# Two decoder layers with 32 SwiGLU experts on one core: a unit of expert weights becomes one expert's whole matrix

## The chip, the cores and the metric

The kernel runs on one core of a Trainium2 chip, in float32. The metric is the device time of one execution in microseconds (us), the median of several runs. The tensor engine (PE) multiplies, the vector engine (DVE) and the scalar engine (ACT) do elementwise work and copies out of PSUM, GpSimd (POOL) does small reciprocal roots, and the sync engine (SP) issues the large loads. Expert weights come from HBM through the core's 16 DMA engines into SBUF.

## The reference, cut to what matters

256 tokens of width 1024 go through two layers. Each layer has a mixer (three kinds in parallel), a cross-attention, and then a mixture of 32 experts, in which a token goes to two:

```python
h = rmsnorm(x, norm3_g[l])
x = x + hierarchical_moe(h, router_wg[l], router_bg[l], router_we[l], router_be[l],
                         exp_w1[l], exp_w3[l], exp_w2[l])

def run(args):
    xb, e = args
    return (jax.nn.silu(xb @ w1[e]) * (xb @ w3[e])) @ w2[e]
```

w1 and w3 are 1024 x 512 per expert, w2 is 512 x 1024: each of the three matrices of an expert has 2 MiB. All 32 experts' weights are read in each layer, 201 MB.

## The kernel before, in words

All engines run one program over `DEPTH` = 2 layers. The dense part of a layer (projections, attentions, state-space mixer) uses weights that SP loads in 18 units (`DENSE`). The expert part goes over 8 quads of 4 experts. With 32 token places per expert (`CAP`), four experts fill the 128 columns of PE side by side: each matmul on expert weights has a 128 x 32 stationary operand (the gathered tokens `XG`, or the hidden values `HIDT`) and a 128 x 512 moving operand (weights), and writes 32 rows of a bank. In the trace each such float32 matmul shows as two records.

Weights of a quad arrive in `MOE_UNITS` = 12 units of 2 MiB, 16 KB in each of the 128 partitions: units 0 to 3 are w1, 4 to 7 are w3, 8 to 11 are w2. In the kernel before, unit i of a matrix holds, for all four experts of the quad, two of the eight 128-row pieces of w1 or w3 (a quarter of w2), so that 4 runs of 4 KB land in each partition. The units go through `ring`, six slots (`SLOTS`), in a loop over quads.

What sets the order:

- **SP** (lines 498 to 524) issues the units in order. Before it loads unit n into a slot, it waits until `units_used` shows that the unit six places earlier has been used by PE (line 522). In the first quad of a layer (`head`), four units go to buffers of the dense part that are free by then (`SPARE_UNITS` 2, 3, 4, 5 in `conv_mem`, `fox_ssd`, `keys_values`, `proj_ht`; line 511), in the order `HEAD_ORDER`; its last two units, 10 and 11, wait for slots 0 and 1 (line 519). The next layer's first dense loads wait for `units_used` too (line 482).
- **PE** (function `quad`, lines 1543 to 1606) waits for a unit in `landed_unit`, runs the 16 matmul records on it, and adds 1 to `units_used` (lines 1580 and 1600). The token gathers of a quad (`gather`, 8 records of 128 x 128 each) stand partly before the first unit and partly between units 0, 1 and 2. After unit 7 come four transposes of the hidden values (line 1590), after unit 11 the scatter (8 records of 128 x 512) that gives the experts' outputs back to the tokens. The helper `mm` is line 1264, so nearly all of PE's work has this line.
- **DVE and ACT** scale the gathered tokens (line 1228), make the SwiGLU product (lines 811, 1236, 1238), copy results (lines 813, 817) and add to the tokens `X` (line 1245). DVE also makes the next quad's selection (line 1147).

Of the kernel before, what the change touches and what calls it, by code (L numbers as in the profile page):

```python
# [24 lines left out]
P = 128  # L25
DEPTH, S, D = 2, 256, 1024
NT = S // P
KC = D // P
# [4 lines left out]
QUAD = 4  # L33
# [150 lines left out]
def trunk(nc, a, out):  # L184
    with ExitStack() as ctx:
# [15 lines left out]
        ring = sb("ring", [P, SLOTS, UNIT])  # L201
# [57 lines left out]
        spare = (conv_mem[:, 0:UNIT], fox_ssd[:, 0:UNIT], keys_values[:, :], proj_ht[:, PROJ_HT - UNIT:])  # L259
# [41 lines left out]
        XG = view(proj, 0, KC, P)  # L301
# [5 lines left out]
        HIDT = view(sq, 512, 4, P)  # L307
# [25 lines left out]
        bank = [ctx.enter_context(nc.psum_tensor(f"bank{b}", [P, 512], F32)) for b in range(NB)]  # L333
        B_GATH, B_SELT, B_UP, B_HIDT, B_DOWN, B_SCAT = (0, 1), 2, (3, 4), 5, (6, 7), (0, 1, 3, 4)
# [4 lines left out]
        landed = [sem(f"landed{s}") for s in range(SLOTS)]  # L339
        spare_in = [sem(f"spare_in{i}", 16) for i in range(SHIFT)]  # L340
# [43 lines left out]
        units_used = sem("units_used")  # L384
# [66 lines left out]
        def landed_by(n, slot, head, l, quads):  # L451

            a_layer = DENSE_TURNS - SHORT[slot]
            layers = l * a_layer + DENSE_TURNS if head else (l + 1) * a_layer
            return layers + quads * MOE_TURNS + sum(moe_slot(m, head) == slot for m in range(n + 1))
# [4 lines left out]
        @block.sync  # L460
        def _(sp):
            for t in range(NT):
                sp.dma_start(X[:, t, :], a["x"][0, t * P:(t + 1) * P, :]).then_inc(x_in[t], 16)
            sp.dma_start(con[:, :], a["const"]).then_inc(const_in, 16)

            def dense(kind, i, l):

                name = {"kv": "xa_wkv", "wq": "xa_wq", "w_out": "w_out", "wo": "xa_wo"}.get(kind, "w_in")
                c0, w, _ = IN_COLS.get(kind, (C_XBC if kind == "xbc" else 0, 512, 0))
                w = W_FV if kind == "fv" else w  # L470
                rows = "a (c p) n -> p (a c) n" if kind in ("w_out", "wo") else "a (p c) n -> p (a c) n"
                v = a[name][bass.ds(l, 1)].rearrange(rows, c=KC)
                return w, v[:, :, c0 + i * 512:c0 + i * 512 + w]

            with sp.Fori(0, DEPTH) as l:

                sp.wait_ge(passes_known, at(passes_known, l, 1))
                quads_before = sp.snap(load_passes(sp, l) * NQ)
                for n, (kind, i) in enumerate(DENSE):
                    if n < SLOTS:  # L480

                        sp.wait_ge(units_used, quads_before * MOE_UNITS + LAST_IN_SLOT[n] + 1)
                        alone(sp)
                    else:

                        sp.wait_ge(*full(last_use(DENSE[n - SLOTS]), l))
                        alone(sp)
                    w, src = dense(kind, i, l)
                    if kind == "fv":
                        place = ring_view(n % SLOTS, IN_COLS["fv"][1])  # L490
                        dt = a["w_in"][bass.ds(l, 1)].rearrange("a (p c) n -> p (a c) n", c=KC)[:, :, C_DT:C_DT + SH]
                        sp.dma_start(place[:, :, w:], dt).then_inc(dt_in, 16)
                    else:
                        place = ring_view(n % SLOTS, w)
                    sp.dma_start(place[:, :, 0:w], src).then_inc(landed[n % SLOTS], 16)

                def quad(q, quads, head=False):
                    for n in HEAD_ORDER if head else range(MOE_UNITS):
                        name, i = ("exp_w1", "exp_w3", "exp_w2")[n // 4], n % 4
                        w = a[name][bass.ds(l, 1)].rearrange("a e k n -> (a e) k n")[bass.ds(q * QUAD, QUAD)]  # L500
                        if name == "exp_w2":
                            src = w.rearrange("e (p c) n -> p e c n", c=4)[:, :, i, :]
                        else:
                            src = w.rearrange("e (p c) n -> p e (c n)", c=KC)[:, :, i * 1024:(i + 1) * 1024]
                        slot = moe_slot(n, head)
                        if slot is None:
                            i = SPARE_UNITS.index(n)

                            sp.wait_ge(*full((("kv", 3, 1), ("ysT", NT - 1), ("xo", 1, XH - 1), ("router",))[i], l))
                            alone(sp)  # L510
                            sp.dma_start(spare[i].rearrange("p (e n) -> p e n", e=QUAD), src).then_inc(spare_in[i], 16)
                            continue
                        if head and n < SLOTS + SHIFT:

                            sp.wait_ge(*full(last_use(DENSE[len(DENSE) - SLOTS + slot]), l))
                            alone(sp)
                        elif head:

                            sp.wait_ge(units_used, quads * MOE_UNITS + MOE_UNITS + slot + 1)
                        else:  # L520

                            sp.wait_ge(units_used, quads * MOE_UNITS + SLOTS + n + 1)
                        sp.dma_start(ring[:, slot, :].rearrange("p (e n) -> p e n", e=QUAD), src  # L523
                                     ).then_inc(landed[slot], 16)
                moe_quads(sp, l, quad, head=lambda q, quads: quad(q, quads, head=True))
            tiles_added = sp.snap(load_passes(sp, DEPTH) * (NQ * NT))
            for t in range(NT):

                sp.wait_ge(x_added, tiles_added + t + 3 - NT)
                alone(sp)  # L530
                sp.dma_start(out[0, t * P:(t + 1) * P, :], X[:, t, :]).then_inc(x_out, 16)
            sp.wait_ge(x_out, 16 * NT)
# [729 lines left out]
        def _(pe):  # L1262
            def mm(dst, lhsT, rhs, start=True, stop=True):
                return nc.tensor.matmul(dst, lhsT, rhs, start=start, stop=stop)  # L1264

            pe.wait_ge(const_in, 16)
            with pe.Fori(0, DEPTH) as l:
# [62 lines left out]
                for i in range(4):  # L1330
                    job = ("xbc", i)
                    w = arrived(("xbc", i // 2))
# [209 lines left out]
                def quad(q, quads, head=False):  # L1542


                    def landed_unit(n):
                        slot = moe_slot(n, head)
                        if slot is None:
                            i = SPARE_UNITS.index(n)
                            pe.wait_ge(spare_in[i], at(spare_in[i], l, 16))
                            return spare[i].rearrange("p (e c n) -> p e c n", e=QUAD, n=512)  # L1550
                        pe.wait_ge(landed[slot], landed_by(n, slot, head, l, quads) * 16)
                        return ring[:, slot, :].rearrange("p (e c n) -> p e c n", e=QUAD, n=512)

                    pe.wait_ge(sel_ready, quads + 1)
                    sel = SEL.rearrange("p t e s -> p t (e s)")
# [13 lines left out]
                    for n in range(8):  # L1569
                        if n < 4:  # L1570

                            pe.wait_ge(XG_ready, quads * 4 + n + 1)
                        u = landed_unit(n)
                        for c in range(2):
                            k = n % 4 * 2 + c
                            for e in range(QUAD):
                                r = slice(CAP * e, CAP * (e + 1))
                                last = mm(bank[B_UP[n // 4]][r, :], XG[:, k, r], u[:, e, c, :],
                                          start=k == 0, stop=k == KC - 1)
                        last.then_inc(units_used, 1)  # L1580
                        if n < 2:
                            gather(n + 2)
                        if n == 3:
                            pe.wait_ge(selg_ready, quads + 1)
                            for t in range(NT):
                                last = nc.tensor.transpose(bank[B_SELT][:, t * P:(t + 1) * P], selg[:, t, :], ident)  # L1586
                            last.then_inc(selt_full, 1)
# [3 lines left out]
                    last.then_inc(hidt_full, 1)  # L1591
                    pe.wait_ge(HIDT_ready, quads + 1)
                    for n in range(4):
                        u = landed_unit(8 + n)
                        for c in range(2):
                            for e in range(QUAD):
                                r = slice(CAP * e, CAP * (e + 1))
                                last = mm(bank[B_DOWN[c]][r, :], HIDT[:, n, r], u[:, e, c, :],
                                          start=n == 0, stop=n == 3)
                        last.then_inc(units_used, 1)  # L1600
                    pe.wait_ge(SELT_ready, quads + 1)
                    pe.wait_ge(YS_ready, quads + 1)
                    for i in range(4):
# [69 lines left out]
```

## Time and profile before

| | before |
|---|---|
| median of 3 runs | 1596.47 us (1595.89 to 1597.43) |
| span of the profiled execution | 1589.7 us |
| PE busy | 1185.8 us, 75% |
| DVE busy | 321.3 us, 20% |
| ACT busy | 221.5 us, 14% |
| moved by DMA | 476.65 MB |

The span runs from the first to the last instruction of the profiled execution. That execution's own device time is not given beside it; the median of the runs is 6.8 us above its span. The page shows the span in 40 slices, the chain of work that ended last, and groups of instructions with the idle time before them; the trace gives the same for any stretch.

### The profile page before, as it was taken

Reading aid. Unit: us, or ns where it says so; the run is one execution under the profiler, and the core shown is the slowest. Engines: PE = TensorE matmul, PEld = TensorE weight load, DVE = VectorE, ACT = ScalarE, POOL = GpSimd, SP = SyncE. Lnnn points to the kernel's source line nnn. Section 1 sums busy time; section 2 is a strip of 40 time slices with the busy share of each in tenths; the row PEclk is TensorE's granted clock in tenths of the full one; section 3 lists DMA queues with packets and bytes.
Section 4 is the critical chain, followed back from the end, with each engine's and each line's share of the span. In section 5 each row is a group of like instructions: output and inputs, shape, how many; then the busy total and the mean of one; then the engine's idle time right before and its main releaser. Section 6 shows DMA issues by size and latency. Waiting matters only on the chain.

```text
span 1589.7 us, 16075 instructions
## 1 busy us (share of the span) xinstructions
PE 1185.8 (75%) x6030; PEld 557.3 (35%) x6031; DVE 321.3 (20%) x835; ACT 221.5 (14%) x491; POOL 43.9 (3%) x81
## 2 busy tenths in 40 slices
PE   6999898977656656566579998988776566566565
PEld 4765544442212212112147645445322122122121
DVE  1125613131101101101021256131311011011010
ACT  4124312110000000000031243122000000000000
POOL 0110000000000000000001100000000000000000
PEclk9999999989989889889889999999798889789888
DMA  9563145379999999999974631453799999999997
GB/s 350 159 212 107 54 158 198 120 274 409 409 410 410 410 410 410 410 410 410 371 250 124 212 107 53 159 211 119 276 410 409 410 409 410 409 410 410 409 410 288
DMA packets 143333, 476.65 MB, mean 300 GB/s; under 512 B 6358, under 2 KB 14894, under 8 KB 143278
## 3 DMA queue, kind: packets, MB, share of 16 engines
q1 hardware_dynamic: 141616, 472.62, 77.0%
q10 hardware_dynamic: 1662, 3.32, 0.6%
q8 instruction: 32, 0.52, 0.1%
q14 instruction: 23, 0.19, 0.0%
HBM read 474.87 MB, written 1.05 MB: 299 GB/s over the span
## 4 chain that ended last, share of the span: by engine, by line
PE 45%; DMA 42%; DVE 5%; issue 3%; SPq 2%; ACT 2%; DVEq 0%; ACTq 0%
PE bank L1264 43%; DMA ring<-exp_w 42%; SPq L523 2%; PE bank L1280 2%; DMA ring<-w_in 1%; DVE X L1245 1%; ACT fox_ssd L817 0%; ACT Y L606 0%; DVE proj_ht L1147 0%; DVE fox_ssd L979 0%; ACT SCO L778 0%; DVE smax L1112 0%; ACT H L766 0%; DVE fox_ssd L1051 0%; DVE proj_ht L1029 0%
## 5 line engine op out<-in xcount | busy, mean ns | idle before, releaser
L1264 PE MATMUL bank<-ring,proj_ht 128*32 128x512 f32 (+3 forms) x2432 | 439.7, 650 | 151.9 <-DMA ring<-exp_w 149.7
L1264 PEld LDWEIGHTS bank<-ring,proj_ht 128*32 128x32 f32 (+1 forms) x2432 | 153.3, 133 | 384.1 <-issue 189.8
L1264 PE MATMUL bank<-ring,SCO 128*32 128x512 f32 x1024 | 165.7, 784 | 114.0 <-DMA ring<-exp_w 112.6
L1264 PEld LDWEIGHTS bank<-ring,SCO 128*32 128x32 f32 x1024 | 34.6, 129 | 234.4 <-DMA ring<-exp_w 148.1
L1264 PE MATMUL bank<-ring,conv_mem 128*128 128x512 f32 x256 | 114.6, 601 | 1.1 <-DVE Y L1061 1.1
L1264 PE MATMUL bank<-ring,H 128*128 128x512 f32 x256 | 112.3, 594 | 2.6 <-ACT H L606 1.5
L1245 DVE TENSOR_TENSOR X<-X,bank 128x512 f32<-128x512 f32 x64 | 44.0, 688 | 338.0 <-PE bank L1264 338.0
L1264 PE MATMUL bank<-proj_ht,H 128*128 128x128 f32 x512 | 73.4, 294 | 23.9 <-DVE proj_ht L1147 23.9
L1264 PEld LDWEIGHTS bank<-proj_ht,H 128*128 128x128 f32 x512 | 64.0, 200 | 62.6 <-DVE proj_ht L1147 35.8
L1264 PE MATMUL bank<-fox_ssd,proj_ht 128*128 128x512 f32 (+1 forms) x160 | 62.5, 600 | 20.6 <-ACT fox_ssd L817 20.6
L1264 PEld LDWEIGHTS bank<-ring,H 128*128 128x128 f32 x256 | 47.8, 190 | 59.5 <-issue 59.4
L1238 DVE SCALAR_TENSOR_TENSOR SCO<-Y,bank 128x512 f32<-128x512 f32 x16 | 16.9, 1054 | 254.7 <-PE bank L1264 254.7
L1264 PEld LDWEIGHTS bank<-ring,conv_mem 128*128 128x128 f32 x256 | 48.3, 192 | 56.8 <-issue 56.6
L1264 PE MATMUL bank<-proj_ht,ring 128*128 128x256 f32 x256 | 55.7, 380 | 0.0
L817 ACT COPY fox_ssd<-bank 128x512 f32<-128x512 f32 x32 | 17.2, 589 | 270.8 <-PE bank L1264 270.8
L1264 PEld LDWEIGHTS bank<-proj_ht,ring 128*128 128x128 f32 x256 | 48.5, 190 | 6.5
L813 ACT COPY SCO<-bank 128x512 f32<-128x512 f32 x16 | 9.4, 585 | 295.1 <-PE bank L1590 295.1
L1228 DVE TENSOR_TENSOR proj_ht<-bank,g 128x256 f32<-128x256 f32 x64 | 27.2, 425 | 111.8 <-PE bank L1264 111.8
L808 ACT COPY proj_ht<-bank 128x256 f32<-128x256 f32 x16 | 6.0, 372 | 313.5 <-PE bank L1586 295.2
L1264 PEld LDWEIGHTS bank<-fox_ssd,proj_ht 128*128 128x128 f32 (+1 forms) x160 | 24.0, 174 | 60.0 <-issue 60.0
L606 ACT COPY proj_ht<-bank 128x512 f32<-128x512 f32 (+2 forms) x32 | 15.4, 480 | 129.1 <-PE bank L1264 128.9
L1236 DVE SCALAR_TENSOR_TENSOR Y<-Y,bank 128x512 f32<-128x512 f32 x16 | 11.0, 688 | 97.8 <-ACT Y L811 97.8
(189 smaller groups left out, 812.1 us busy)
## 6 DMA issues: line engine op xcount, KB each, us to landing
ring<-exp_w SPq DMA_DIRECT2D x184, 2048.0 KB, 23.7
ring<-w_in SPq DMA_DIRECT2D x8, 2048.0 KB, 17.8
ring<-xa_wkv SPq DMA_DIRECT2D x8, 2048.0 KB, 11.9
ring<-w_out SPq DMA_DIRECT2D x4, 2048.0 KB, 9.8
ring<-xa_wq SPq DMA_DIRECT2D x4, 2048.0 KB, 9.2
ring<-xa_wo SPq DMA_DIRECT2D x4, 2048.0 KB, 7.7
ring<-w_in SPq DMA_DIRECT2D x6, 1024.0 KB, 12.3
conv_mem<-exp_w SPq DMA_DIRECT2D x2, 2048.0 KB, 12.7
```

The costliest lines, as they stand in the source:

```text
L523: sp.dma_start(ring[:, slot, :].rearrange("p (e n) -> p e n", e=QUAD), src).then_inc(landed[slot], 16)
L606: nc.scalar.copy(dst, src).then_inc(read(job), 1)
L808: nc.scalar.copy(SELT, bank[B_SELT][:, 0:S]).then_inc(SELT_ready, 1)
L813: nc.scalar.copy(HIDT, bank[B_HIDT][:, :].rearrange("p (c s) -> p c s", c=4)).then_inc(HIDT_ready, 1)
L817: last = nc.scalar.copy(YS[:, n * 512:(n + 1) * 512], bank[B_DOWN[n]][:, :])
L1228: v.tensor_tensor(XG[:, 2 * i:2 * i + 2, :], view(bank[B_GATH[i % 2]], i // 2 * 2 * P, 2, P), bc(my_gain[:, 2 * i:2 * i + 2], 2, P), ALU.m ...
L1236: step(v.scalar_tensor_tensor(SIGM, SIGM, 1.0, bank[B_UP[0]][:, :], ALU.add, ALU.mult))
L1238: v.scalar_tensor_tensor(HID, SIGM.rearrange("p (q c) -> p c q", c=4), 0.5, bank[B_UP[1]][:, :].rearrange("p (q c) -> p c q", c=4), ALU.mu ...
L1245: last = v.tensor_tensor(x, x, bank[B_SCAT[i]][:, :], ALU.add)
L1264: return nc.tensor.matmul(dst, lhsT, rhs, start=start, stop=stop)
L1280: last = nc.tensor.transpose(bk(job)[0:src.shape[1], i * P:i * P + src.shape[0]], src, ident[0:src.shape[0], 0:src.shape[0]])
```

## The change

A unit is now one expert's whole matrix, contiguous in HBM, and lands as one run of 16 KB in each partition. PE needs all four experts for a matmul step, so it waits for the four units of a matrix ahead of the first step, and gives the four slots back together after the last. The matmuls themselves, their number, shapes and order over k and the experts, stay as they were; so do the slots, the order in which units are loaded, and SP's wait conditions.

```diff
                 def quad(q, quads, head=False):
                     for n in HEAD_ORDER if head else range(MOE_UNITS):
-                        name, i = ("exp_w1", "exp_w3", "exp_w2")[n // 4], n % 4
-                        w = a[name][bass.ds(l, 1)].rearrange("a e k n -> (a e) k n")[bass.ds(q * QUAD, QUAD)]
-                        if name == "exp_w2":
-                            src = w.rearrange("e (p c) n -> p e c n", c=4)[:, :, i, :]
-                        else:
-                            src = w.rearrange("e (p c) n -> p e (c n)", c=KC)[:, :, i * 1024:(i + 1) * 1024]
+                        name = ("exp_w1", "exp_w3", "exp_w2")[n // QUAD]
+                        w = a[name][bass.ds(l, 1)].rearrange("a e k n -> (a e) k n")[bass.ds(q * QUAD + n % QUAD, 1)]
+                        src = w.rearrange("e (p c) n -> p (e c n)", p=P)
...
-                        sp.dma_start(ring[:, slot, :].rearrange("p (e n) -> p e n", e=QUAD), src
+                        sp.dma_start(ring[:, slot, :], src
                                      ).then_inc(landed[slot], 16)
...
+                    def landed_matrices(matrix, width):
+
+                        return [landed_unit(QUAD * matrix + e, width) for e in range(QUAD)]
...
-                        u = landed_unit(n)
+                        if n % 4 == 0:
+                            u = landed_matrices(n // 4, 512)
                         for c in range(2):
                             k = n % 4 * 2 + c
                             for e in range(QUAD):
                                 r = slice(CAP * e, CAP * (e + 1))
-                                last = mm(bank[B_UP[n // 4]][r, :], XG[:, k, r], u[:, e, c, :],
+                                last = mm(bank[B_UP[n // 4]][r, :], XG[:, k, r], u[e][:, k, :],
                                           start=k == 0, stop=k == KC - 1)
-                        last.then_inc(units_used, 1)
+                        if n % 4 == 3:
+                            last.then_inc(units_used, QUAD)
...
                     for n in range(4):
-                        u = landed_unit(8 + n)
+                        if n == 0:
+                            u = landed_matrices(2, 1024)
                         for c in range(2):
                             for e in range(QUAD):
                                 r = slice(CAP * e, CAP * (e + 1))
-                                last = mm(bank[B_DOWN[c]][r, :], HIDT[:, n, r], u[:, e, c, :],
-                                          start=n == 0, stop=n == 3)
-                        last.then_inc(units_used, 1)
+                                last = mm(bank[B_DOWN[c]][r, :], HIDT[:, n, r],
+                                          u[e][:, n, c * 512:(c + 1) * 512], start=n == 0, stop=n == 3)
+                        if n == 3:
+                            last.then_inc(units_used, QUAD)
```

SP, in the loop over quads, the last four units of a quad. Before (each row `L522` is the arithmetic of a wait, each DMA one unit of 4 runs of 1024 numbers per partition):

```order
L522 REGISTER_ALU
L523 DMA ring<-exp_w 128x4x1024
L522 REGISTER_ALU
L523 DMA ring<-exp_w 128x4x1024
L522 REGISTER_ALU
L523 DMA ring<-exp_w 128x4x1024
L522 REGISTER_ALU
L523 DMA ring<-exp_w 128x4x1024
```

And now:

```order
L519 REGISTER_ALU
L520 DMA ring<-exp_w 128x4096
L519 REGISTER_ALU
L520 DMA ring<-exp_w 128x4096
L519 REGISTER_ALU
L520 DMA ring<-exp_w 128x4096
L519 REGISTER_ALU
L520 DMA ring<-exp_w 128x4096
```

The loads stand in the same places with one long run each; 166 rows of SP before and after.

PE, the same loop, w3 and w2 of a quad (`SCO` holds the hidden values, `proj_ht` the gathered tokens; rows L1551 before and L1550 after are in `landed_unit`; here a float32 matmul counts once). Before:

```order
L1551 ISA
L1264 MATMUL bank<-ring,proj_ht 32x512 x16
L1551 ISA
L1264 MATMUL bank<-ring,proj_ht 32x512 x16
L1590 MATMUL bank<-con,SCO 128x128 x4
L1264 MATMUL bank<-ring,SCO 32x512 x16
L1551 ISA
L1264 MATMUL bank<-ring,SCO 32x512 x16
```

And now:

```order
L1550 ISA x2
L1261 MATMUL bank<-ring,proj_ht 32x512 x32
L1596 MATMUL bank<-con,SCO 128x128 x4
L1550 ISA
L1261 MATMUL bank<-ring,SCO 32x512 x32
```

The waits that stood among the matmuls of a matrix have moved ahead of all 32 of them.

## Rows read from the trace of the kernel before

**Rows 1.** The page: DMA share and GB/s in 40 slices of the span.
```profile
DMA  9563145379999999999974631453799999999997
GB/s 350 159 212 107 54 158 198 120 274 409 409 410 410 410 410 410 410 410 410 371 250 124 212 107 53 159 211 119 276 410 409 410 409 410 409 410 410 409 410 288
```

**Rows 2.** The page: the chain that ended last, by engine.
```profile
PE 45%; DMA 42%; DVE 5%; issue 3%; SPq 2%; ACT 2%; DVEq 0%; ACTq 0%
```

**Rows 3.** Timeline, PE in quad 1 of layer 1 (start us, us, engine, line, operation).
```profile
483.90 3.67 PE L1264 MATMUL bank<-fox_ssd,proj_ht 128*128 128x512 f32 x8 [1.29 <-ACT fox_ssd L817]
...
506.28 3.43 PE L1264 MATMUL bank<-ring,proj_ht 128*32 128x512 f32 x16 [2.73 <-DMA ring<-exp_w]
...
511.41 1.92 PE L1264 MATMUL bank<-ring,proj_ht 128*32 128x512 f32 x16 [1.70 <-DMA ring<-exp_w]
...
545.34 3.67 PE L1264 MATMUL bank<-fox_ssd,proj_ht 128*128 128x512 f32 x8 [1.29 <-ACT fox_ssd L817]
```

**Rows 4.** DMA packets from 28 to 36, 38 to 44 and 500 to 520 us.
```profile
DMA packets 1518, 3.09 MB, mean 386 GB/s; under 512 B 16, under 2 KB 16, under 8 KB 1517
...
DMA packets 2070, 2.09 MB, mean 348 GB/s; under 512 B 32, under 2 KB 2069, under 8 KB 2070
...
DMA packets 2062, 8.19 MB, mean 410 GB/s; under 512 B 62, under 2 KB 62, under 8 KB 2062
```

**Rows 5.** DMA from 5.5 to 6.5 us, SP's queue (packets, MB): it loads `con`.
```profile
q1 hardware_dynamic: 43, 0.22, 59.0%
```

**Rows 6.** A unit issued at 317.96 us; DMA just after (PEclk, DMA share, GB/s last).
```profile
317.96 0.37 SPq L523 DMA_DIRECT2D ring<-exp_w  x1
...
DMA to landing us min/median/max: 8.2/8.2/8.2
...
318.00:319.20 1.20, 1.20 (x13) 1.20 (x12) 0.53 (x1) 0.58 (x1) 0.00 (x0) 1.00 0.30 38
```

**Rows 7.** The load into `proj_ht` issued at 324.45 us: time to landing.
```profile
DMA to landing us min/median/max: 8.0/8.0/8.0
```

**Rows 8.** Timeline of quad 0 of layer 1, and unit 4 of quad 1.
```profile
335.69 1.99 PE L1264 MATMUL bank<-ring,proj_ht 128*32 128x512 f32 x16
...
337.75 103.36 SPq L523 DMA_DIRECT2D ring<-exp_w  x22
...
343.38 1.90 PE L1264 MATMUL bank<-fox_ssd,proj_ht 128*32 128x512 f32 x16
...
345.86 1.92 PE L1264 MATMUL bank<-keys_values,proj_ht 128*32 128x512 f32 x16
...
349.32 3.62 PE L1264 MATMUL bank<-ring,proj_ht 128*32 128x512 f32 x32
...
355.44 8.77 PE L1264 MATMUL bank<-ring,SCO 128*32 128x512 f32 x64 [0.67 <-ACT SCO L813]
...
372.72 1.92 PE L1264 MATMUL bank<-ring,proj_ht 128*32 128x512 f32 x16
...
383.41 1.93 PE L1264 MATMUL bank<-ring,proj_ht 128*32 128x512 f32 x16 [0.80 <-DMA ring<-exp_w]
```

**Rows 9.** Stretches: us, busy PE, PEld, DVE, ACT, POOL; PEclk, DMA share, GB/s.
```profile
356.50:359.70 3.20, 3.20 (x19) 0.64 (x13) 0.00 (x0) 0.00 (x0) 0.00 (x0) 0.50 1.03 415
359.90:364.20 4.30, 4.30 (x43) 1.04 (x32) 0.00 (x0) 0.00 (x0) 0.00 (x0) 1.00 1.02 412
...
506.60:509.90 3.30, 3.11 (x16) 0.44 (x8) 0.00 (x0) 0.00 (x0) 0.00 (x0) 0.50 1.02 408
```

**Rows 10.** Timeline at the end of layer 1 and the start of layer 2.
```profile
786.45 0.62 SPq L492 DMA_DIRECT2D ring<-w_in  x1
...
787.77 1.92 PE L1264 MATMUL bank<-ring,SCO 128*32 128x512 f32 x16 [1.59 <-DMA ring<-exp_w]
...
790.98 3.67 PE L1264 MATMUL bank<-fox_ssd,proj_ht 128*128 128x512 f32 x8 [1.29 <-ACT fox_ssd L817]
...
810.16 5.22 PE L1264 MATMUL bank<-ring,proj_ht 128*128 128x268 f32 x22
```

More of the change, by code:

```diff
@@ L510, in quad @@
                             alone(sp)
-                            sp.dma_start(spare[i].rearrange("p (e n) -> p e n", e=QUAD), src).then_inc(spare_in[i], 16)
+                            sp.dma_start(spare[i], src).then_inc(spare_in[i], 16)
                             continue
@@ L1542, in quad, with landed_unit @@
                 def quad(q, quads, head=False):
-                    def landed_unit(n):
+                    def landed_unit(n, width):
                         slot = moe_slot(n, head)
@@ L1549, in landed_unit @@
                             pe.wait_ge(spare_in[i], at(spare_in[i], l, 16))
-                            return spare[i].rearrange("p (e c n) -> p e c n", e=QUAD, n=512)
-                        pe.wait_ge(landed[slot], landed_by(n, slot, head, l, quads) * 16)
-                        return ring[:, slot, :].rearrange("p (e c n) -> p e c n", e=QUAD, n=512)
+                            u = spare[i]
+                        else:
+                            pe.wait_ge(landed[slot], landed_by(n, slot, head, l, quads) * 16)
+                            u = ring[:, slot, :]
+                        return u.rearrange("p (c n) -> p c n", n=width)
+                    def landed_matrices(matrix, width):
+                        return [landed_unit(QUAD * matrix + e, width) for e in range(QUAD)]
                     pe.wait_ge(sel_ready, quads + 1)
```

## The prediction

> **What bounds the kernel now.** I read the page's slices first. In the dense part of a layer the DMA engines are half idle; in the expert part, slices 10 to 19 and 30 to 39, they move 409 to 410 GB/s without a break [rows 1]. The chain of waits agrees: PE 45%, DMA 42% [rows 2], PE's share lying mostly in the dense part. The timeline of a quad shows it at close range: PE runs 16 records on a unit, then waits for the next, every 5.12 us (506.28 to 511.41) [rows 3]. A quad, from scatter to scatter, takes 545.34 - 483.90 = 61.44 us, which is 12 units of 5.12 us. So in the expert part only two things can change the time: how fast the DMA engines move bytes, and whether they ever run out of issued loads. They do not now, since each unit's slot is given back 2 to 3.5 us after it landed.
>
> **Term 1, the longer runs.** The mean packet was 3.09 MB / 1518 = 2 KB at 386 GB/s, 1 KB at 348, 4 KB at 410 [rows 4]. Over 16 engines that is 47.1 ns for 1 KB, 84.9 ns for 2 KB, 159.8 ns for 4 KB. Each doubling leaves a fixed part: 2 x 47.1 - 84.9 = 9.3 ns, 2 x 84.9 - 159.8 = 10.0 ns. I take 9.3. If a run of 16 KB is one packet, it takes 4 x 159.8 - 3 x 9.3 = 611 ns, so 429 GB/s, and a unit (2.097 MB) 4.90 us instead of 5.12. Does a long run stay whole? While SP loaded `con`, its queue moved 0.22 MB in 43 packets, 5.1 KB each [rows 5]: nothing cuts at 4 KB there. The bounds are 4.90 us and, if runs are cut, 5.12 us. Alone this term would give 12 x 0.22 = 2.6 us per quad, 42 us over 16 quads.
>
> The Trainium skill (DMA: Bandwidth & Descriptors, "Where 436 GB/s comes from") puts the ceiling of this path at 435 GB/s. By that a unit takes 4.82 us at best and the sum below would be some 7 us lower; the 429 is under it.
>
> **Term 2, slots given back by four.** The ring has six slots. When the last unit of a matrix has landed, four slots hold that matrix, and only two loads are issued beyond it. Nothing more can be issued until PE has finished all 64 records. Two units keep the DMA engines busy for 9.8 us (10.2 at the old rate). A load issued to idle engines landed 8.2 us and 8.0 us after its issue (38 GB/s were moving in the first 1.2 us) [rows 6, 7]. Against 5.12 us of pure transfer that is 2.9 us of start and finish; I add 0.1 us from PE's last record to SP's issue (335.69 + 1.99 = 337.68, issue at 337.75 [rows 8]). So, with T the time from a matrix's landing to its last matmul, the next matrix lands after the larger of T + 3.0 and two units, plus two units more.
>
> What is T? The nearest rows are in quad 0, where the units lay ready. For w1 the records ran from 335.69 to 343.38 + 1.90 = 345.28: 9.6 us, with two gathers and their copies in between. For w3: 345.86 to 349.32 + 3.62 = 352.94, 7.1 us. For w2: 8.77 us [rows 8], because the granted clock was 0.50 (1.2 GHz) in its first part and 1.00 (2.4 GHz) after [rows 9]. Sixteen records take 1.92 us at full clock and 3.43 us at half [rows 3]. After a wait of 2.73 us the clock fell to 0.50 within the burst at 506.28 [rows 3, 9]. In the changed kernel PE idles far longer ahead of w3 and w2, so I take 8.8 for both, and 9.6 for w1, since its gathers run shortly before. The bounds are 9.6, 7.1, 7.1 at full clock throughout, and 11.3, 10.5, 10.5 if half clock lasts twice as long in each as in the burst at 355.44.
>
> A quad then takes (9.6 + 3.0) + (8.8 + 3.0) + (8.8 + 3.0) = 36.2 us, plus six units of 4.90 = 29.4: 65.6 us against 61.4. At 5.12 us a unit: 66.9.
>
> **Term 3, the edges of a layer.** Quad 0's units 10 and 11 are issued when w1 is finished, 345.4 instead of 337.75, and land at 353.2 and 358.1. So w2 starts at 358.1 instead of 355.44 [rows 8] and ends at 366.9. The four loads that wait for it follow at 367.0, and quad 1's w1 is complete at 367.0 + 2.9 + 2 x 4.90 = 379.7. Before, it was one unit ahead of the wait that ended at 383.4 [rows 8], 378.3: +1.4. Six whole quads follow: 6 x 4.2 = +25.2. In the last quad w1 to w3 to w2 takes 12.6 + 11.8 + 4 x 4.90 = 44.0 instead of 8 x 5.12 = 41.0: +3.0. Then the last burst is 8.8 us, where one unit took 2.0 [rows 10]: +6.8, with nothing to hide it, as copies, scatter and the next layer's norms follow on it. Sum 36.4 us per layer, 73 us for both.
>
> **What costs nothing.** The next layer's first loads were issued at 786.45, 4.5 us ahead of the last scatter; now they come 1.2 us ahead of it, since the slots are given back at the burst's end. PE first uses them near 810 [rows 10], 19 us after the scatter; this slack covers 3.3 us, and if it were gone the price would be those 3.3 us once. SP's queue has the same loads in the same order, so nothing is moved past another load. Gathers, transposes and DVE's work are as before: after w2's burst, copies, scatter, selection and gather take 372.7 - 364.2 = 8.5 us [rows 8], and 8.8 + 8.5 is less than the 21.6 us until the next w1 is complete.
>
> **The sum.** The profiled span is 1589.7 us; with 73 it is 1663. The median of the runs stands 6.8 us above this span, so I forecast 1596.5 + 73 = **1669 us**.
>
> **Rivals.**
>
> - *Runs are cut or gain nothing* (20%). Rows 5 speak against it. A quad takes 66.9 us, the layer's edges +2.2, +3.9 and +6.8, so 2 x (6 x 5.5 + 12.9) = 92: 1688 us.
> - *The clock stays half for longer* (15%). In the bursts after 10 us of idling T may be 11.3, 10.5 and 10.5: a quad 14.3 + 13.5 + 13.5 + 29.4 = 70.7, +9.3. Layer: 6 x 9.3 + 3 + 6.4 + 8.5 = 74, so 1744 us in full; half of the effect gives 1706. For it: a wait of under 3 us is followed by half clock now [rows 3, 9]. Against it: full clock came back inside the burst at 355.44.
> - *The burst keeps full clock* (10%). T is 9.6, 7.1, 7.1. A quad takes 12.6 + 10.1 + 10.1 + 29.4 = 62.2, +0.8; the edges -0.3, +1.3 and +5.1. Sum 2 x 11 = 22: 1618 us. The Trainium skill (TensorE: Matmul & The Clock Gate, "HAM oscillation") advises to run all k-tiles before the next DMA wait so that PE stays warm, which would speak for this change; here the half-clock row ahead of it makes me give it little.
> - *Faster: the restart is hidden* (5%). The place is SP's wait at line 523. If part of the 2.9 us is hidden because four loads are issued at once, the DMA engines never starve; this decides when T + restart is under 9.8 us, so with a restart under 1.0 us at w3 and w2 and 0.2 us at w1. Then a quad takes 12 x 4.90 = 58.8, -2.6; last quad 39.2 instead of 41.0, -1.8; last burst +6.8. 2 x (-15.6 - 1.8 + 6.8) = -21: 1575 us. Against it stand 8.0 and 8.2 us from issue to landing.
> - *The longer runs are slower* (5%): at 380 GB/s a unit takes 5.5 us, a quad 36.2 + 33.0 = 69.2, the sum near 126: 1722 us.
>
> **How the numbers follow.** My forecast has 45%, with its own range 1650 to 1685. A measurement of this kernel can tell about 0.2% (3 us) from no change. Faster: 5% from the hidden restart and 1% for a full clock together with a better rate than 429. Within 0.2%: 2%, where a full clock meets a short restart. Slower: the rest, 92%. The range is 1618 to 1712: it holds the forecast, the cut runs, the full clock, and the smaller half of the clock rival; outside are the faster case, the slower runs and a clock at half for most of the bursts.
>
> **What would show each step.** DMA packets of 16 KB and about 429 GB/s in a stretch in which DMA is busy. The DMA share in the expert slices below 1.00, with gaps after each pair of units, three in a quad. Bursts of 64 records on PE near 8.8 us for w3 and w2, and waits of PE on `ring<-exp_w` of about 13 us. Scatter to scatter 65.6 us. SP waiting for PE at its line for the loads, with 8 us from issue to landing of the first of four. The forecast is wrong if the DMA share stays at 1.03 through a quad (no starving), if packets are still 4 KB, or if the 64 records take over 10 us.

## The result and the profile after

The changed kernel takes 1719.6 us (median of 4 runs, 1716.2 to 1721.6) against 1596.2 for the kernel before, measured beside it: 1.077 times the kernel before, 95% interval 1.075 to 1.0785. The sign and the mechanism came out as forecast, the size did not: 123 us slower where 73 were forecast, and 8 us beyond the upper end of the range.

The page of the changed kernel, the lines that answer to [rows 1] and [rows 2]:

```profile
span 1718.4 us, 16107 instructions
...
PE   6999898764655645546579999988745546455455
...
PEclk9999999887878868878789999998868778688787
DMA  9472133589898898988673621335988888999885
GB/s 350 121 241 103 50 134 160 196 345 375 352 376 368 373 390 353 376 366 351 261 251 115 228 99 49 147 147 196 371 350 352 365 363 355 384 375 379 367 349 215
...
PE 59%; DMA 32%; DVE 3%; issue 2%; SPq 1%; ACT 1%; DVEq 0%; ACTq 0%
```

In the expert slices the DMA engines moved an unbroken 410 GB/s before; now it is mostly 350 to 390, with busy digits of 8 and 9. The chain has moved from DMA (42% before) to PE (59%), although PE has the same work.

SP's own waits, from the same trace (who waited for whom: us in total, times, longest us):

```profile
SPq L520 <- PE bank L1261: 900.1, 46, 23.8
```

SP waits 46 times for PE at its line for the loads, close to once per matrix (48), up to 23.8 us each. PE waits for the landings in turn. The timeline of quad 2 of layer 1 with the start of the next (start us, us), which answers to [rows 3]. The quads of a layer are numbered 0 to 7 by the order of their scatters; [rows 3] lie in quad 3 by this count, not in quad 1:

```profile
442.44 3.67 PE L1261 MATMUL bank<-fox_ssd,proj_ht 128*128 128x512 f32 x8 [1.28 <-ACT fox_ssd L814]
447.79 2.05 PE L1261 MATMUL bank<-proj_ht,H 128*128 128x128 f32 x16 [1.68 <-DVE proj_ht L1144]
454.30 3.42 PE L1261 MATMUL bank<-ring,proj_ht 128*32 128x512 f32 x16 [4.46 <-DMA ring<-exp_w]
457.65 1.16 PE L1261 MATMUL bank<-proj_ht,H 128*128 128x128 f32 x8
458.74 1.92 PE L1261 MATMUL bank<-ring,proj_ht 128*32 128x512 f32 x16
460.59 1.16 PE L1261 MATMUL bank<-proj_ht,H 128*128 128x128 f32 x8
461.68 3.64 PE L1261 MATMUL bank<-ring,proj_ht 128*32 128x512 f32 x32
...
478.44 8.45 PE L1261 MATMUL bank<-ring,proj_ht 128*32 128x512 f32 x64 [12.76 <-DMA ring<-exp_w]
...
499.84 9.68 PE L1261 MATMUL bank<-ring,SCO 128*32 128x512 f32 x64 [11.13 <-DMA ring<-exp_w]
510.81 3.67 PE L1261 MATMUL bank<-fox_ssd,proj_ht 128*128 128x512 f32 x8 [1.28 <-ACT fox_ssd L814]
...
522.86 3.27 PE L1261 MATMUL bank<-ring,proj_ht 128*32 128x512 f32 x16 [4.68 <-DMA ring<-exp_w]
```

Scatter to scatter is 510.81 - 442.44 = 68.4 us (forecast 65.6, before 61.4). T, the time from a matrix's landing to its last matmul, is read here from its first record to its last: 461.68 + 3.64 - 454.30 = 11.0 us for w1, 8.45 for w3, 9.68 for w2. The waits on `ring<-exp_w` are 12.8 and 11.1 us.

Stretches of this kernel: the burst of w2 that began at 431.37, first and later part; then the gap in the loads after a w1 (busy times; PEclk, DMA share, GB/s last):

```profile
431.40:437.00 5.60, 5.60 (x28) 1.52 (x32) 0.00 (x0) 0.00 (x0) 0.00 (x0) 0.51 1.01 430
437.00:441.00 4.00, 4.00 (x40) 1.08 (x32) 0.00 (x0) 0.00 (x0) 0.00 (x0) 1.00 0.69 295
...
465.50:467.00 1.50, 0.19 (x2) 0.00 (x0) 0.37 (x1) 0.87 (x2) 0.00 (x0) 1.00 0.62 131
```

While loads are in flight they move at 430 GB/s; 429 was worked out from [rows 4]. Half clock holds for 5.6 us of the burst, and DMA runs dry before the burst has ended. SP's issues after the burst of w2 (it ended at 431.37 + 9.79 = 441.16), and the time from the first of them to its landing:

```profile
441.42 1.49 SPq L520 DMA_DIRECT2D ring<-exp_w  x3
...
DMA to landing us min/median/max: 7.8/7.8/7.8
```

So 0.26 us from PE to the issue, and 7.8 to the landing, of which 4.9 are transfer. After the burst of w3 before it (issue at 418.63) and the w1 after it (465.38) the first load landed 7.7 and 8.0 us after its issue, and SP issued it 0.06 us after PE's last record. From the end of w2 at 441.16 to the next w1 at 454.30 are 13.1 us: two units of 4.9 and 3.3 us of restart, not 3.0.

### The profile page after: what moved, and what is told of

Same layout as the page of the kernel before. It is cut to its first block, busy times and chain, and to the rows that moved or that the text cites. A ratio compares the mean times of both kernels' runs of the same rounds, so it can differ in the third digit from the quotient of the medians.

```text
span 1718.4 us, 16107 instructions
## 1 busy us (share of the span) xinstructions
PE 1172.9 (68%) x6030; PEld 581.4 (34%) x6031; DVE 321.3 (19%) x835; ACT 221.9 (13%) x491; POOL 43.5 (3%) x81
## 4 chain that ended last, share of the span: by engine, by line
PE 59%; DMA 32%; DVE 3%; issue 2%; SPq 1%; ACT 1%; DVEq 0%; ACTq 0%
PE bank L1261 57%; DMA ring<-exp_w 31%; PE bank L1277 2%; SPq L520 1%; DMA ring<-w_in 1%; ACT Y L603 0%; DVE fox_ssd L976 0%; ACT SCO L775 0%; ACT H L763 0%; DVE fox_ssd L1048 0%; DVE proj_ht L1026 0%; ACT proj_ht L697 0%; DVE smax L1109 0%; DVE fox_ssd L1050 0%; DVE proj_ht L934 0%
## 5 line engine op out<-in xcount | busy, mean ns | idle before, releaser
L1261 PE MATMUL bank<-ring,proj_ht 128*32 128x512 f32 (+3 forms) x2432 | 446.9, 652 | 243.5 <-DMA ring<-exp_w 241.1
L1261 PEld LDWEIGHTS bank<-ring,proj_ht 128*32 128x32 f32 (+1 forms) x2432 | 167.6, 138 | 452.7 <-issue 440.7
L1261 PE MATMUL bank<-ring,SCO 128*32 128x512 f32 x1024 | 154.2, 769 | 163.6 <-DMA ring<-exp_w 163.6
L1261 PEld LDWEIGHTS bank<-ring,SCO 128*32 128x32 f32 x1024 | 42.1, 137 | 265.0 <-issue 265.0
L1261 PE MATMUL bank<-fox_ssd,proj_ht 128*128 128x512 f32 (+1 forms) x160 | 73.8, 602 | 20.5 <-ACT fox_ssd L814 20.5
L1261 PEld LDWEIGHTS bank<-ring,H 128*128 128x128 f32 x256 | 47.8, 190 | 59.5 <-issue 59.4
L1225 DVE TENSOR_TENSOR proj_ht<-bank,g 128x256 f32<-128x256 f32 x64 | 27.2, 425 | 199.9 <-PE bank L1261 199.9
L1261 PE MATMUL bank<-keys_values,proj_ht 128*128 128x256 f32 (+1 forms) x96 | 33.7, 488 | 2.0 <-DVE proj_ht L853 2.0
## 6 DMA issues: line engine op xcount, KB each, us to landing
ring<-w_out SPq DMA_DIRECT2D x4, 2048.0 KB, 10.2
```

The lines of the kernel that those rows point to most:

```text
L1225: v.tensor_tensor(XG[:, 2 * i:2 * i + 2, :], view(bank[B_GATH[i % 2]], i // 2 * 2 * P, 2, P), bc(my_gain[:, 2 * i:2 * i + 2], 2, P), ALU.m ...
```

## The experiments

### Grouping alone, with 4 KB runs

The kernel before, with PE's waits and the return of slots in fours (`group4k`):

```diff
-                        u = landed_unit(n)
+                        if n % 4 == 0:
+                            four = [landed_unit(n + j) for j in range(4)]
+                        u = four[n % 4]
...
-                        last.then_inc(units_used, 1)
+                        if n % 4 == 3:
+                            last.then_inc(units_used, 4)
```

(and likewise for w2). Three dots mark lines left out.

> The kernel before with its 4 KB runs; PE alone is changed: it waits for the four units of a matrix and gives their slots back together. Theory A (starving by slots given back in fours): each matrix costs T + about 3.3 us + two units, with T 11.0, 8.5 and 9.7 us as in the changed kernel, so a quad takes 29.2 + 9.9 + 6 x 5.12 = 69.8 us and the whole some 20 us more than the changed kernel's 1719.6, about 1740. Theory B (what costs is the long run itself: a slower restart or uneven DMA engines): a quad stays near 61.4 us plus little, the whole below 1640.

It took 1747.9 us, 1.095 times the kernel before (1.093 to 1.096). From its scatters at 445.02 and 869.22 us the six quads between take 70.7 us each. Its timeline shows the same bursts behind the same waits:

```profile
483.07 8.94 PE L1264 MATMUL bank<-ring,proj_ht 128*32 128x512 f32 x64 [13.11 <-DMA ring<-exp_w]
...
505.36 9.74 PE L1264 MATMUL bank<-ring,SCO 128*32 128x512 f32 x64 [11.51 <-DMA ring<-exp_w]
```

The loss comes with PE's grouping alone, with not one long run in the kernel. The long runs help: the changed kernel is 28 us faster than this one. The forecast of 1740 us and 69.8 us per quad was 8 and 0.9 us low.

### Waiting for four, giving back one by one

The same kernel, but `units_used` rises after each unit's 16 records, as in the kernel before (`wait4k`; only the first half of the diff above).

> As the last, but each unit's slot is given back after its own 16 matmul records, as before. Theory A: the first slot comes back under 3.5 us after the matrix landed, with 10.2 us of loads still in flight, so the DMA engines never run dry: a quad takes 61.4 us, the whole about 1612 (the last burst of each layer is some 7 us longer). Rival: waiting for four units costs by itself (PE starts late and everything shifts): a quad takes 65 us or more, the whole 1650 to 1740.

It took 1612.4 us, 1.010 times the kernel before (1.008 to 1.011), and a quad 61.44 us. Twenty microseconds of it and the next w3 burst:

```profile
500.00:520.00 20.00, 11.01 (x93) 4.92 (x91) 2.72 (x6) 0.87 (x2) 0.00 (x0) 0.89 1.03 410
...
523.57 9.85 PE L1264 MATMUL bank<-ring,proj_ht 128*32 128x512 f32 x64 [10.58 <-DMA ring<-exp_w]
```

A burst of 64 records in 9.85 us, longer than in the changed kernel, behind a wait of 10.6 us, and yet DMA moves 410 GB/s without a gap. So neither the wait for four nor the burst's length costs anything in a quad here, where the first slot comes back early. `group4k` and `wait4k` differ in nothing but the returns, so the difference, 135 us, is the price of giving back in fours. What is left, 16 us, lies at the edges of the layers: in layer 1 the first scatter comes 2.2 us and the second 9.9 us later than before, and the six quads that follow take the same time as before.

### Full clock in the bursts

The changed kernel with filler matmuls, whose result nobody reads, ahead of the waits (`warm`):

```diff
                     def landed_matrices(matrix, width):
 
+                        for _ in range((4, 13, 11)[matrix]):
+                            mm(bank[B_HIDT][:, :], ident, con[:, 0:512])
                         return [landed_unit(QUAD * matrix + e, width) for e in range(QUAD)]
```

> The changed kernel with 4, 13 and 11 filler matmuls (128 x 512, two records each, into the bank of the hidden values, never read) ahead of the waits for w1, w3 and w2. Theory A with the clock: the bursts run at full clock, T is 9.6, 7.1 and 7.1 us, and a quad takes 23.8 + 9.9 + 29.4 = 63.1 us instead of 68.3, in both layers. If the clock is not what sets T, a quad stays at 68 us. The first quads have no waits and get longer by the fillers, up to 20 us per layer, so the whole is no measure; near 1665.

```profile
539.84 1.92 PE L1261 MATMUL bank<-ring,proj_ht 128*32 128x512 f32 x16 [1.13 <-DMA ring<-exp_w]
...
549.57 11.32 PE L1261 MATMUL bank<-con 128*128 128x512 f32 x26
562.50 7.07 PE L1261 MATMUL bank<-ring,proj_ht 128*32 128x512 f32 x64 [1.60 <-DMA ring<-exp_w]
```

The rows are its timeline: w1, fillers, w3. The burst of w3 takes 7.07 us at full clock. From w1 to w3 are 22.7 us (24.1 in the changed kernel). The six whole quads of layer 1 take 63.1 to 66.7 us, 64.2 on the mean, against 68.3 in the changed kernel and 63.1 expected; the granted clock in them was 0.95 to 1.00. It is one run of 1706.3 us, where about 1665 was expected. Its first scatter comes at 391.9 instead of 372.0 us, and the first quad carries fillers with no wait to hide them, so only the quads compare. The half clock costs 4 us per quad on the mean and 5 in the best quad, and the formula of T plus restart plus two units holds within 1.2 us for a third set of T. Even near full clock the quad is slower than before.

### 16 KB runs, two experts per step

Does the long run pay if the slots come back in time? In `pairs16` PE takes two units per step:

```diff
-                        return [landed_unit(QUAD * matrix + e, width) for e in range(QUAD)]
+                        return [landed_unit(QUAD * matrix + e, width) for e in pair]
...
+                        for pair in ((0, 1), (2, 3)):
...
-                        if n % 4 == 3:
-                            last.then_inc(units_used, QUAD)
+                                if n == 3:
+                                    last.then_inc(units_used, 2)
```

> The changed kernel, but PE takes two units (two experts) per step: 32 records of two column groups, then gives two slots back. Theory A: at most two slots are held, four units (19.6 us) stay in flight, T for a pair is 6.9 us at full clock, so the DMA engines never run dry and a quad takes 12 x 4.90 = 58.8 us: the whole 1570 to 1590, faster than the kernel before. Theory B: the long runs still cost, no faster than before. Rival C: two column groups at a time make PE the bound (6 x 6.9 + gathers, copies and scatter = 55 us at full clock, over 60 at half), a quad takes 60 to 66 us.

```profile
490.00:550.00 60.00, 50.79 (x246) 17.70 (x245) 6.94 (x12) 2.53 (x5) 0.00 (x0) 1.00 1.01 428
```

The stretch lies in two quads of layer 1: 428 GB/s without a gap. Five of the twelve quads 2 to 7 took 58.7 us, where theory A had 58.8; the mean was 59.0 in layer 1 and 59.7 in layer 2. Yet the whole took 1610.2 us, 1.0085 times the kernel before (1.006 to 1.011), outside the expected 1570 to 1590. The expectation had left out the first quad of a layer, where all units but the last two lie ready and PE is the bound. A step of 32 records on two column groups takes as long as 64 records on four:

```profile
460.98 7.06 PE L1261 MATMUL bank<-ring,proj_ht 128*32 128x512 f32 x32
```

The first scatter came at 380.4 us instead of 365.5.

In `head4_pairs` the first quad goes by four experts, the others by pairs:

```diff
+                    steps = ((0, 1, 2, 3),) if head else ((0, 1), (2, 3))
...
-                        for pair in ((0, 1), (2, 3)):
+                        for pair in steps:
```

> As pairs16, but in the first quad of a layer, whose units lie ready, PE takes four experts per step as in the changed kernel; the other seven quads go by pairs. In pairs16 the first scatter came 14.9 us later than in the kernel before (380.4 against 365.5), and the quads after it took 58.7 us. If that edge is PE at two column groups with nothing to wait for, it shrinks to the changed kernel's 6.5 us (372.0), twice 8.4 us less: 1610 - 17 = 1593, the same as before within the uncertainty. If the edge has another cause (late loads of units 10 and 11), it stays near 1610.

The first scatter moved from 380.4 to 371.4 us and the whole to 1594.3, 0.998 times the kernel before (0.996 to 1.000): the same. So 9.0 of the 14.9 us of that edge were PE's two column groups, and in layer 2 the time from the last scatter of layer 1 to the first of layer 2 fell by 14.1. In the traces, the twelve quads 2 to 7 gain 23 us against the kernel before; the time ahead of the first scatters (13.5 us) and the two quads 1 (12 us) cost about as much.

### 8 KB runs, two units per step, four experts

In `halves8` a unit is half of k of one matrix for two experts. Two units hold all four experts over half of k, so PE keeps its four column groups and gives slots back in twos:

```diff
+                        h = n % 4 // 2
+                        src = w.rearrange("e (p c) n -> p e (c n)", p=P)[:, :, h * 2048:(h + 1) * 2048]
...
-                        if n % 4 == 3:
-                            last.then_inc(units_used, QUAD)
+                        if n % 2 == 1:
+                            last.then_inc(units_used, 2)
```

> A unit is half a matrix of two experts (two runs of 8 KB per partition); PE takes two units per step, all four column groups over half of k, 32 records, and gives two slots back. Theory A: T is 3.5 to 5.5 us with at least two more units in flight beyond those just landing (four slots free of the step), so no starving; 8 KB packets take 2 x 159.8 - 9.3 = 310 ns, 423 GB/s, a unit 4.96 us, a quad 59.5 us: -1.9 us in each of 14 quads, against a last burst longer by 3 us and a first quad later by up to 4 us per layer: 1596 - 27 + 14 = 1583, with 1572 to 1590. If giving slots back in twos starves the DMA engines already, a quad stays at 61 us or more and the whole at 1600 or above.

It took 1584.8 us, 0.991 times the kernel before (0.989 to 0.994): faster than both kernels, by under 1% against the kernel before, and where 1583 was expected. A stretch, the packets in its first 20 us, and the timeline of w3:

```profile
500.00:560.00 60.00, 37.52 (x237) 13.16 (x230) 6.70 (x12) 2.53 (x5) 0.00 (x0) 0.83 1.01 422
...
DMA packets 1102, 8.47 MB, mean 424 GB/s; under 512 B 68, under 2 KB 68, under 8 KB 68
```

```profile
452.96 5.00 PE L1262 MATMUL bank<-ring,proj_ht 128*32 128x512 f32 x32 [5.07 <-DMA ring<-exp_w]
462.90 5.15 PE L1262 MATMUL bank<-ring,proj_ht 128*32 128x512 f32 x32 [4.94 <-DMA ring<-exp_w]
```

DMA moves 422 GB/s with its engines always busy. A step of 5.0 us, partly at half clock, is over long before the two units behind it have landed, one step per 9.94 us. A mean quad takes (788.83 - 430.67) / 6 = 59.7 us; 59.5 was expected.

## Why the prediction was right and wrong

**Right: term 1.** Runs stay whole: between 500 and 520 us of `pairs16`, which has the changed kernel's loads, 8.49 MB came in 582 packets, 64 of them under 512 B, so the other 518 had 16 KB on the mean. For the 429 GB/s worked out from [rows 4] 430 and 428 were measured, and for 8 KB 422 to 424 where 423 was expected. By `group4k` the long run is worth 28 us inside the starving kernel.

**Right: the mechanism of term 2.** `group4k` and `wait4k` differ only in when slots come back, and have the whole loss between them. The wait named there (SP for PE, once per matrix) is in the trace.

**Wrong: the size of term 2.** This is the step that failed: 123 us instead of 73, because T, the restart and the edges were each priced too low.

| us added, both layers | forecast | measured |
|---|---|---|
| quads 2 to 7 (12 of them) | 50.4 | 84.7 |
| quad 1 of each layer | 17.0 | 28.0 |
| all ahead of the first scatter of each layer | 5.4 | 15.8 |
| sum | 73 | 128.7 (spans) |

The measured values are differences of scatter starts between the two traces. With 0.2 us after the last scatter's start they make the spans' 1718.4 - 1589.7 = 128.7. Between the medians it is 123: the device times of the runs lie 1.8 to 1.9 us above their spans, so the profiled execution of the kernel before took about 1591.5 us (an estimate), some 5 us less than its median.

- *T.* Forecast 9.6 + 8.8 + 8.8 = 27.2, measured 11.0 + 8.45 + 9.7 = 29.1. The error was to take one burst, the row of 8.77 us in [rows 8], for both w3 and w2, and to give w1 no half clock because its gathers run shortly before. It waits 4.46 us after them, and its first 16 records took 3.42 us, where 1.92 is full clock; the burst of w2 had half clock for 5.6 us. That is 1.9 us per quad, 23 us over 12 quads. `warm` shows what is at stake: 4 us per quad on the mean between this kernel and one near full clock. The rival on a clock that stays half for longer had T at 32.3 us, 5.1 above the forecast. The measured 1.9 is over a third of that, so part of this rival belonged in the forecast.
- *The restart.* The start of the first load was right: it landed 7.7 to 8.0 us after its issue, 2.8 to 3.1 beyond a unit's 4.9, where 2.9 was forecast. What was too small is the rest. SP took 0.26 us instead of 0.1 after w2, and PE's first record came about 0.15 us after the second load's landing (issued at 442.06, landed 12.1 us later, record at 454.30). From 499.84 + 9.68 to the next w1 at 522.86 are 13.3 us, 3.5 beyond two units; the three matrices together give 68.4 - 29.1 - 29.4 = 9.9 instead of 9.0. Over 12 quads that is 11 us.
- *Quad 1 and the edges.* The error of T and the restart, 2.8 us, recurs in each quad 1. The prediction listed no small loads. They were there before, too, but then the weights on their way covered them; behind a starved ring they delay a matrix that PE waits for. SP issued units 10 and 11 at 347.68 and 348.2, together with ACT's loads of 0.6 MB for the next layer's parameters. The second landed after 13.9 us, where it was 12.1 us at 442.06, and w2 started at 362.2 instead of 358.1 (2.3 us of that came from the later issue). The load of `mem`, 1 MB, was issued at 370.89, at the very moment at which the ring was refilled (371.01); the second unit took 14.5 us and quad 1's w1 started at 386.30 instead of 379.7. The added 1.8 and 2.4 us fit the bytes: at 430 GB/s 0.6 MB take 1.4 us and 1 MB takes 2.4 (estimates). A further part of the time ahead of the first scatters lies in the dense work itself, which the change doesn't touch: the first record on an expert weight came 2.4 us later in layer 1, and in layer 2 5.5 us later, counted from the last scatter of layer 1. In layer 1 there is a stretch at half clock:

```profile
265.00:273.00 8.00, 6.58 (x26) 5.45 (x27) 3.10 (x10) 1.80 (x6) 1.01 (x1) 0.58 1.00 430
```

The same stretch had 1.00 in the kernel before. It is not a mark of the grouping: `wait4k` and `warm` had 0.59 and 0.60 there, `group4k` and `pairs16` 1.00. What decides it stays open.

**The rivals.** Runs that are cut, slower long runs and a hidden restart fell at once with the profile (430 GB/s while loads are in flight, and 3.3 us of restart). The burst at full clock (62.2 us a quad forecast) does not happen by itself, and the rule of the Trainium skill (TensorE: Matmul & The Clock Gate, "HAM oscillation") did not hold in its consequence here: all k-tiles stand between two waits, and the waits ahead of them are the longer for it, so PE did not stay warm. In the timeline of quad 2 the first 16 records on w1 took 3.42 us instead of 1.92, and the bursts of w3 and w2 8.45 and 9.68 instead of 7.07: 5.5 us lost to half clock. That is hardly less than before, where 4 of a quad's 12 groups of 16 records took 3.4 to 3.5 us instead of 1.92. There it hid behind the loads; now it lies on the path. With the clock forced up in `warm` a quad took 64.2 us on the mean.

## What to carry to other kernels

In a ring that feeds a DMA-bound loop, count what is still in flight when a step's operands have landed: it must cover the step's whole time up to the return of its first slot, plus the restart (here 3.3 us). In the two kernels that starved, 8.5 to 11 us and the restart stood against 9.8 or 10.2 us of loads; in `wait4k` it was 3.4 and the restart against 10.2, in `halves8` 5.0 and the restart against almost 20 (four units of 4.97). The border itself was not tried. If the loads in flight don't cover it, the difference is paid at every step, and here the better rate paid back only 28 of the 135 us. Longer runs are worth having (4 to 8 KB gave 3% of rate here, 8 to 16 KB 1.4% more), so choose the longest run whose slots still come back in small lots: 8 KB in twos beat both 4 KB one by one and 16 KB in fours. A burst that follows a long wait is to be priced with half clock in its first part, for w1 as for the others (64 records took 8.5 to 9.8 us here, 7.07 at full clock), and a load that was hidden in a busy queue has to be priced anew where the queue runs dry.

## What was unexpected of the hardware

The rates by run length fell on one line: 348, 386, 410 GB/s for 1, 2 and 4 KB [rows 4], then 422 to 424 for 8 KB and 428 to 430 for 16 KB, as a fixed 9.3 ns per packet gives (worked out from the first two or three and right for the last two). And 32 records on two column groups took 7.06 us in `pairs16`, as long as 64 on four (7.07 in `warm`), both at full clock: the groups that are left empty save nothing.
